# A fused two-block layer on one core: the first weight tile rounded by VectorE, x's second quarter turned behind the first products, the third tile rounded in two chunks

## The reference

```python
h = rmsnorm(x, norm_mix[layer])                       # x: 1 x 256 x 1024
(q, kc, vc, ks, vs, kw, vw, nsa_g, rq, rk, rv, rg, gate_a, gate_b) = jnp.split(
    h @ w_in[layer], offsets, axis=-1)                # w_in: 1024 x 5400
```

## Time and profile before

| | |
|---|---|
| time, median of 3 runs | 949.09 us (949.04 to 949.36) |
| the profiled execution | 948.88 us |
| its span, first to last instruction | 947.1 us |
| PE busy | 940.2 us, 99% of the span, 6904 matmuls |
| VectorE, ScalarE, GpSimd busy | 709.4, 563.5, 134.6 us |
| DMA | 170.39 MB, mean 180 GB/s |
| granted TensorE clock | 1.000 |
| chain that ended last | PE 98%, VectorE 1% |

### The profile page before, as it was taken

The page is one execution under the profiler, slowest core; times in us unless marked ns, Lnnn a source line. Parts: engine busy times, 40 slices in busy tenths (PEclk is TensorE's granted clock), DMA queues, the critical chain, the costliest instruction groups (busy, mean ns, idle before and its releaser), DMA issues.

```text
span 947.1 us, 17052 instructions
## 1 busy us (share of the span) xinstructions
PE 940.2 (99%) x6904; PEld 868.0 (92%) x6904; DVE 709.4 (75%) x947; ACT 563.5 (59%) x861; POOL 134.6 (14%) x186
## 2 busy tenths in 40 slices
PE   9999999999999999999999999999999999999997
PEld 7877999989999999989988999998998899999997
DVE  5768875779778887878876787776667468777777
ACT  6577564557666566666865674545455455455544
POOL 3000001005223220404000001100000032121211
PEclk9999999999999999999999999999999999999999
DMA  9964447545666566656565365555655346565661
GB/s 316 307 219 150 133 112 179 176 159 185 199 198 199 182 197 200 185 158 198 148 186 170 99 204 175 176 184 172 196 163 168 122 156 192 181 197 188 194 207 67
DMA packets 133807, 170.39 MB, mean 180 GB/s; under 512 B 5824, under 2 KB 98064, under 8 KB 133728
## 3 DMA queue, kind: packets, MB, share of 16 engines
q1 hardware_dynamic: 131552, 165.08, 56.7%
q10 hardware_dynamic: 1536, 2.77, 0.8%
q0 software_dynamic: 640, 1.44, 0.7%
HBM read 168.22 MB, written 1.05 MB: 179 GB/s over the span
## 4 chain that ended last, share of the span: by engine, by line
PE 98%; DVE 1%; DMA 0%; issue 0%; POOLq 0%; ACT 0%; ACTq 0%; DVEq 0%; POOL 0%
PE ps L441 23%; PE ps L409 15%; PE ps L410 15%; PE ps L413 15%; PE ps L391 4%; PE ps L584 3%; PE ps L923 3%; PE ps L927 3%; PE ps L922 3%; PE ps L867 2%; PE ps L863 2%; PE ps L864 2%; PE ps L616 1%; PE ps L619 1%; PE ps L474 1%; PE ps L615 1%
## 5 line engine op out<-in xcount | busy, mean ns | idle before, releaser
L1814 DVE TENSOR_TENSOR parts<-raws,parts 128x1024 fp32r<-128x1024 f32 (+3 forms) x307 | 363.7, 1201 | 120.6 <-ACT parts L1244 119.7
L1244 ACT ACTIVATE parts<-raws 128x1024 fp32r<-128x1024 f32 (+3 forms) x307 | 308.5, 1028 | 120.1 <-PE ps L413 51.1
L409 PE MATMUL ps<-room_r,parts 128*128 128x256 f32 x1248 | 308.6, 281 | 0.0
L410 PE MATMUL ps<-room_r,parts 128*128 128x256 f32 x1248 | 306.4, 279 | 0.0
L409 PEld LDWEIGHTS ps<-room_r,parts 128*128 128x128 f32 x1248 | 234.3, 188 | 2.2 <-issue 0.8
L410 PEld LDWEIGHTS ps<-room_r,parts 128*128 128x128 f32 x1248 | 235.0, 188 | 1.2
L441 PE MATMUL ps<-parts,room_r 128*128 128x512 f32 (+1 forms) x960 | 225.4, 392 | 0.0
L441 PEld LDWEIGHTS ps<-parts,room_r 128*128 128x128 f32 x960 | 175.6, 188 | 40.0 <-issue 0.4
L413 PE MATMUL ps<-room_r,parts 128*128 128x256 f32 x1248 | 196.5, 279 | 0.0
L413 PEld LDWEIGHTS ps<-room_r,parts 128*128 128x128 f32 x1248 | 167.7, 188 | 0.0
L1848 DVE TENSOR_TENSOR room_r<-room,room_r 128x512 fp32r<-128x512 f32 (+2 forms) x75 | 53.6, 721 | 31.0 <-ACT room_r L1542 10.1
(11 more groups left out here) (252 smaller groups left out, 1159.1 us busy)
## 6 DMA issues: line engine op xcount, KB each, us to landing
raws<-in_w_in SPq DMA_DIRECT2D x99, 512.0 KB, 4.4
raws<-in_w_ffn_in SPq DMA_DIRECT2D x44, 512.0 KB, 4.7
raws<-in_w_up SPq DMA_DIRECT2D x32, 512.0 KB, 3.9
raws<-in_w_down SPq DMA_DIRECT2D x32, 512.0 KB, 3.8
raws<-in_w_ffn_out SPq DMA_DIRECT2D x22, 512.0 KB, 4.4
raws<-in_w_xkv SPq DMA_DIRECT2D x16, 512.0 KB, 3.9
raws<-in_w_out SPq DMA_DIRECT2D x8, 512.0 KB, 4.6
raws<-in_w_up_ssd SPq DMA_DIRECT2D x8, 512.0 KB, 5.1
```

The lines of the kernel that those rows point to most:

```text
L409: e.matmul(ps, wh, hT[0][:, k, :], start=k == 0, stop=False)
L410: e.matmul(ps, wh, hT[1][:, k, :], start=False, stop=False)
L1244: e.activation(t.h, t.raw, ACT.Copy).then_inc(s["hi"], 1)
L1814: e.tensor_tensor(t.l, t.raw, t.h.bitcast(F32), ALU.subtract).then_inc(s["lo"], 1)
```

## The change

It has three parts. (1) The first tile's rounding goes from ScalarE (an activation) to VectorE (a `tensor_copy`), which then takes its remainder as before; ScalarE begins with the first quarter, and waits for `hi` before it rounds the second tile, so that the count stays in order. (2) `first_block` yields after its two first products, chunk 0 with the rounded first tile; the second quarter is turned there, where it was turned ahead of the block. `idle(2)` becomes `idle(1)`. (3) The third tile is rounded by two activations, one per slice of depth, the first counted by a new semaphore `third_hi`; the block's products with that tile's rounded part go by slices (chunk 2 for both banks, then chunk 3), where they went by banks. VectorE waits for `third_hi` too.

```diff
@@ first_block
                 for t in range(2):
                     product(w0, 0, t, 0, w0.h, True)
+                yield
                 need(s["lo"], w0.i + 1)
...
                 w2 = weight(w[2 * P:4 * P, 0:n], 2, n)
+                need(s["third_hi"], 1)
+                need(s["x_even_hi"], 2)
+                for t in range(2):
+                    e.matmul(psum[:, own[t], :], xT[0][:, 2, t * P:t * P + P], w2.h[:, 0, :], start=False, stop=False)
                 need(s["hi"], w2.i + 1)
-                need(s["x_even_hi"], 2)
                 need(s["xT_hi"], 2)
                 for t in range(2):
-                    product(w2, 2, t, 0, w2.h)
+                    e.matmul(psum[:, own[t], :], xT[0][:, 3, t * P:t * P + P], w2.h[:, 1, :], start=False, stop=False)
                 yield
@@ tensor
             x_quarter(0)
-            idle(2)
-            x_quarter(1)
+            idle(1)
 
             w_in = a["w_in"][0]
             units = first_block("qkv", w_in)
+            next(units)
+            x_quarter(1)
             next(units)
@@ scalar
-            round_tile()
             quarter_rounded(0)
+            hi = 1
+            e.wait_ge(s["hi"], 1)
             round_tile()
             quarter_rounded(1)
-            round_tile()
+            third = tiles[hi]
+            e.wait_ge(landed[third.slot], third.load)
+            e.activation(third.h[:, 0, :], third.raw[:, 0, :], ACT.Copy).then_inc(s["third_hi"], 1)
+            e.activation(third.h[:, 1, :], third.raw[:, 1, :], ACT.Copy).then_inc(s["hi"], 1)
+            hi += 1
@@ vector
+            first = tiles[0]
+            e.wait_ge(landed[first.slot], first.load)
+            e.tensor_copy(first.h, first.raw).then_inc(s["hi"], 1)
             rest_of_tile()
             quarter_rest(0)
             rest_of_tile()
             quarter_rest(1)
+            e.wait_ge(s["third_hi"], 1)
             rest_of_tile()
```

More of the change, by code:

```diff
@@ L42 @@
     "act_step", "dve_step", "pool_step",
-    "final_col", "gain2", "sumsq", "zsq", "rstd", "z", "zrstd", "mlp_rstd", "x_scale", "spread", "xT_hi", "xT", "x_even_hi", "x_even", "y",
+    "final_col", "gain2", "sumsq", "zsq", "rstd", "z", "zrstd", "mlp_rstd", "x_scale", "spread", "xT_hi", "xT", "x_even_hi", "x_even", "third_hi", "y",
     "zeros", "red", "trig", "q_rot", "r_rot", "gsig", "again", "no_keys", "win_end", "windows", "pc_sub", "pc_exp", "pc", "nmax", "weighed",
```

## The result

The changed kernel is slower by a little: median 950.26 us over 20 executions against 949.31 over 20 of the kernel before, ratio 1.0017 with the interval 1.0011 to 1.0023. The forecast was 950.0. The median hides what the executions do: those of the changed kernel fall into two groups with nothing between.

A forecast was written before the change was run, and what follows sets the result against it. TensorE's gapless instruction stream was taken to bound the kernel, so lateness at its head lasts to the end. The late table load adds 0.88 us to 949.09, nothing given back: 949.97, so 950.0 us, range 949.2 to 950.9.

The forecast's parts named there:

- The load behind the second wait: ScalarE's head: the table load moves from 1.74 us to behind chunk 0's transposes, about 4.73 us; activation 1.30 us after it.
- the first product: TensorE's head: starts at 6.54 us, after x_even_hi at 6.49 and 0.05 for the release.
- the copy: VectorE's rounding of the first tile: 0.41 us from the landing at about 4.71, hidden behind the table load.
- no wait in the middle: TensorE's long dense stretch: the later order of PSUM banks costs 0, with 0.3 us either way in the range.
- The drain: ScalarE's table load: the skill's switch of 2.66 us includes 1.38 of drain, giving 951.3 us; the forecast left it out.
- the sum: Whole kernel: TensorE 0.88 us later from the head on, nothing given back, 949.97 us, so 950.0.
- rival 2: TensorE's head: clock falls in the longer pause, slow stretch of 3.6 us returns once, 1.8 us more, 951.8 us; chance 0.07.
- within: Whole kernel: a change within 0.2%, 1.9 us, which a measurement can't tell from no change; chance 0.89.
- Rival 1: ScalarE's head: the table load stays early, first products at 5.24 to 5.45, 0.3 us won, 948.8 us; chance 0.06.
- Rival 3: TensorE's middle: bank order or a shifted load opens waits or takes some away, 949.4 to 950.9 us; chance 0.04.

The follow-up runs named there:

- the repeat: The changed kernel timed again with no edit, beside the kernel before: median 951.56 us, ratio 1.0017 (1.0008 to 1.0025).
- the six profiles: Six more profiles of the changed kernel, no edit, one execution each: 950.0, 950.01, 949.95, 950.07, 953.0 and 951.36 us.
- the kernel before with the wait: Kernel before, idle(2) left out, second quarter's transposes waiting for the second tile's rounding: 951.88 us; with idle(9) filling the pause 950.56 us.

## Why the prediction was right and wrong

**The path, right.** The load behind the second wait at 4.62 (forecast 4.73), the first product at 6.54 (6.54), the copy 0.43 us (0.41), hidden behind the load; no wait in the middle; 0.86 later between the two profiles (0.88), and 0.7 to 0.8 by the lower group's medians. Moving the load by the waits alone (949.17) or by hand (948.97) takes this cost away, so the cause of the lower group is shown, not only its place.

**What was luck.** The exact 6.54 is two misses that cancel: the load came 0.11 early, as the four transposes took 0.69 where 0.96 stood, and from the activation's end to the product 0.14 passed where I had 0.05; in the other lower profiles the first product came at 6.68 to 6.80. And the median of 950.26 stands by the forecast of 950.0 only because 11 of 20 executions fell in the lower group. In the repeat five of 11 did, and the median, 951.56, is outside the range that I gave.

**The drain.** By the Trainium skill (ScalarE: Activation LUTs, "What ACT_TABLE_LOAD costs") it would have been 951.3. The load was followed by its activation after 1.30 us again, and the trace decides against the drain here.

**The step that failed: the sum has nothing for TensorE's clock.** It stood apart, as rival 2, held to be another outcome with a chance of 0.07. But it isn't a case that holds or doesn't; it comes in some executions and not in others, 17 of 37 of the changed kernel. So the sum was to have 0.86 plus about half of 1.8, some 1.7 us, and the ratio says 1.6 (0.0017 of 949.31; 1.0 to 2.2 by its interval). The reason against it, "the stream behind it is dense", was wrong: dense work at 1.2 GHz ran for 2.8 and 6.0 us in two profiles. And "the granted clock reads 1.00 in each stretch, the head too" did not say what I took from it: in the execution of 953.0 that column reads 1.00 over the slow products too. The durations of one shape tell the level there, as the earlier trace rows did.

Rival 2 was right in what would show it, products much further apart behind the pause, and its price of 1.8 is the distance of the two groups. Its mechanism was another. I had the clock fall in a longer pause, and the slow stretch of the start come back once; in both upper profiles of the changed kernel it had not risen when the pause began, and the slow stretch behind the pause was 2.8 and 6.0 us, not 3.6. That the price fits is thus luck in part. The rows could have warned: I read the rise as about 4.65 us from one execution, 0.35 ahead of the pause that the change makes, and left no room for it to come later. The Trainium skill (TensorE: Matmul & The Clock Gate, "What's actually happening") says that the point of the rise differs between runs of one kernel, by half a microsecond either way, since the chip's watch on TensorE's activity doesn't start with the kernel. The runs agree that it differs: in the profile after it came during the first transposes (4.06 to 4.75), in the fourth of the six profiles only after 5.65. The 9.6 and 12.9 of two others lie far outside of what that section gives. I had taken the state from it and not this.

**What a measurement tells.** I wrote 0.2%, 1.9 us; with 20 executions a side the interval was 0.06% either way. A shift of 0.88 us alone would have been told from no change, and the chance of 0.89 for "within" rested on the coarser figure.

**The rivals.** Rival 1's event didn't come, and its price was too good: 0.3 won in the sum, 0.1 to 0.2 in the run that made it come, since VectorE's copy follows the tile's landing (4.98 there, 4.71 in the sum). Rival 3 is out: the middle is as dense as before, the kernels that move the load alone keep the new order of banks and lose nothing, and whole or in chunks the third tile gives the same time.

**Open.** What sets in one execution when the clock rises was not controlled by any run: a pause ahead of the first product makes a late rise frequent (upper executions: 17 of 37, against two of 33 in the kernels with the waits swapped and with the load by hand, in chunks or whole), but one came without it (the 951.0 of the swapped waits). Nor is it known why the kernel with part 1 undone has three of 11 in an upper group behind a pause of 0.5 us.

## What to carry to other kernels

An activation that waits for two things has its table load behind the second of the waits in the code, however long the engine was idle: issue the load by hand early, or let the second wait be the one that ends first. A pause put where TensorE's clock rises costs something in some executions and nothing in others, so a price for it needs a frequency, several executions and not one profile, and the level is read from the duration of one shape. An instruction moved behind a product in TensorE's stream inherits everything that the product waits for.

## What the runs showed of the hardware

A table load ahead of an activation with two waits began when the second of them in the code ended: at 4.62 us behind the transposes, at 3.82 behind the gain's landing once the two were swapped. It took 1.28 us in every profile.

The clock's rise and its fall are two costs. Pauses of 1.36 to 1.56 us after the rise did no harm in five profiles; in one profile a pause of 2.49 us brought a fall from 1.00 to 0.50 for over 3 us of dense work. A pause of 1.15 us begun before the rise left TensorE at the low level until 9.6 or 12.9 us in two profiles of three. In one execution of another kernel it stayed there until near 9.9 us with no pause but 0.53 us ahead of the transposes. With zero matmuls in the pause no execution was in the upper group, in the changed kernel and in the kernel before with the wait (none of 11 each); they cost time themselves in two profiles where they outlasted the wait.
